# The order of VectorE and ScalarE in a gated-linear-attention mixer: weight subtractions and small steps change places

## The reference

```python
h = rmsnorm_2(x, mix_norm[l])
z = h @ w_in[l]
q_a, k_a, v_a, q_b, k_b, v_b, r_b, g_lr, gate_a, gate_b = split_cols(z, IN_SPLITS)
o_a = swa_attention(...)                    # sliding window, 8 heads
o_b = gla_attention(...)                    # gated linear attention, 4 heads
o_b = rmsnorm_2(o_b, gla_out_norm[l]...) * jax.nn.silu(r_b)
y_a = o_a @ w_proj_a[l]
y_b = o_b @ w_proj_b[l]
merged = jax.nn.sigmoid(gate_a) * y_a + jax.nn.sigmoid(gate_b) * y_b
x = x + merged @ w_out[l]
```

## Time and profile before

| | before |
|---|---|
| time of the runs, us | 2284.65, 2286.96, 2285.08 (median 2285.08) |
| the profiled execution | 2284.65 us, span of its records 2282.9 us |
| TensorE matmul | busy 2272.3 us of the span |
| TensorE weight load | busy 1931.9 us |
| VectorE | busy 1537.2 us |
| ScalarE | busy 1241.8 us |
| granted TensorE clock | 9 tenths or more in all 40 slices |
| DMA | mean 182 GB/s |

### The profile page before, as it was taken

The page is one execution under the profiler, slowest core; times in us unless marked ns, Lnnn a source line. Parts: engine busy times, 40 slices in busy tenths (PEclk is TensorE's granted clock), DMA queues, the critical chain, the costliest instruction groups (busy, mean ns, idle before and its releaser), DMA issues.

```text
span 2282.9 us, 29070 instructions
## 1 busy us (share of the span) xinstructions
PE 2272.3 (100%) x11756; PEld 1931.9 (85%) x11756; DVE 1537.2 (67%) x2156; ACT 1241.8 (54%) x1484; POOL 0.2 (0%) x4
## 2 busy tenths in 40 slices
PE   8999999999999999999999999999999999999999
PEld 7887888888888788888888888888888888888887
DVE  6764566765774466775776588767657747876773
ACT  6644445554653444654554576555555537754652
POOL 0000000000000000000000000000000000000000
PEclk9999999999999999999999999999999999999999
DMA  7556454564555455455555553645555555345553
GB/s 254 199 196 223 142 190 171 198 207 162 197 190 202 144 179 204 166 195 184 189 198 195 192 166 102 212 163 188 203 183 183 188 183 188 103 157 195 192 185 129
DMA packets 175802, 416.52 MB, mean 182 GB/s; under 512 B 16658, under 2 KB 21394, under 8 KB 175668
## 3 DMA queue, kind: packets, MB, share of 16 engines
q1 hardware_dynamic: 175380, 414.52, 53.0%
q10 hardware_dynamic: 288, 0.14, 0.0%
HBM read 413.55 MB, written 1.05 MB: 182 GB/s over the span
## 4 chain that ended last, share of the span: by engine, by line
PE 97%; DVE 1%; DMA 1%; ACT 1%; issue 0%; SPq 0%; DVEq 0%; ACTq 0%
PE psum L656 27%; PE psum L592 17%; PE psum L594 16%; PE psum L593 16%; PE psum L657 14%; PE psum L624 2%; PE psum L928 1%; PE psum L756 1%; DVE split_w L1581 0%; DMA raw<-t_gate_up_1a_dram 0%; PE psum L906 0%; DMA x<-x_dram 0%; PE psum L773 0%; ACT split_w L1129 0%; PE psum L897 0%
## 5 line engine op out<-in xcount | busy, mean ns | idle before, releaser
L1581 DVE TENSOR_TENSOR split_w<-raw,split_w 128x2048 fp32r<-128x2048 f32 (+2 forms) x408 | 886.4, 2178 | 308.8 <-ACT split_w L1129 307.8
L656 PE MATMUL psum<-xt,split_w 128*128 128x512 f32 x2816 | 982.0, 393 | 2.6 <-DVE split_w L1581 1.8
L1129 ACT ACTIVATE split_w<-raw 128x2048 fp32r<-128x2048 f32 (+2 forms) x408 | 741.0, 1824 | 325.2 <-PE psum L594 295.3
L657 PE MATMUL psum<-xt,split_w 128*128 128x256 f32 x2816 | 786.6, 279 | 0.0
L656 PEld LDWEIGHTS psum<-xt,split_w 128*128 128x128 f32 x2816 | 527.2, 187 | 123.4 <-DVE split_w L1581 2.2
L657 PEld LDWEIGHTS psum<-xt,split_w 128*128 128x128 f32 x2816 | 531.4, 189 | 0.3
L592 PE MATMUL psum<-split_w,xt 128*128 128x512 f32 (+1 forms) x736 | 291.1, 395 | 0.0
L594 PE MATMUL psum<-split_w,xt 128*128 128x512 f32 (+1 forms) x736 | 283.8, 386 | 0.0
L593 PE MATMUL psum<-split_w,xt 128*128 128x512 f32 (+1 forms) x736 | 283.6, 385 | 0.0
L592 PE MATMUL psum<-split_w,ht_hi 128*128 128x512 f32 x700 | 273.0, 390 | 0.0
L594 PE MATMUL psum<-split_w,ht_lo 128*128 128x512 f32 x700 | 272.5, 389 | 0.0
(11 more groups left out here) (272 smaller groups left out, 1731.1 us busy)
## 6 DMA issues: line engine op xcount, KB each, us to landing
raw<-w_in_dram SPq DMA_DIRECT2D x180, 512.0 KB, 4.4
raw<-t_gate_up_1b_dram SPq DMA_DIRECT2D x88, 512.0 KB, 4.1
raw<-t_gate_up_2a_dram SPq DMA_DIRECT2D x88, 512.0 KB, 4.1
raw<-t_gate_up_2b_dram SPq DMA_DIRECT2D x88, 512.0 KB, 4.1
raw<-t_gate_up_1a_dram SPq DMA_DIRECT2D x85, 512.0 KB, 4.2
raw<-ffn_w_down_dram SPq DMA_DIRECT2D x80, 512.0 KB, 4.3
raw<-w_a_dram SPq DMA_DIRECT2D x40, 512.0 KB, 4.1
raw<-w_b_dram SPq DMA_DIRECT2D x40, 512.0 KB, 4.2
```

Source lines behind the costliest of these rows:

```text
L656: nc.tensor.matmul(bank, whi[:, slot, w], xt[:, c, :, :], start=c == 0, stop=False)
L657: last = nc.tensor.matmul(bank[:, 0:T], wlo[:, slot, w], xt_hi[:, c, :], start=False, stop=c == DC - 1)
L1129: nc.scalar.activation(whi[:, u % HL, first:n], raw[:, r, first:n], ACT.Copy).then_inc(hi_done, 1)
L1581: nc.vector.tensor_tensor(wlo[:, u % HL, first:n], raw[:, r, first:n], whi[:, u % HL, first:n], ALU.subtract).then_inc(w_ready, 1)
```

## The change

Nothing is added or removed; eight calls change places, in the program of VectorE and of ScalarE. On VectorE, `turned(2)` goes ahead of `split(u0 + 23)`, `merge("a", 0, ...)` ahead of `split(u0 + 24)`, `merge("a", 1, ...)` ahead of `turned(3)` and both ahead of `split(u0 + 26)`, and `split(u0 + 27)` goes behind `gated(3)`, `out_norm()` and both `out_scaled()`; `split(u0 + 23)` goes behind `decayed(3, ...)` and `gated(1)` as well. On ScalarE, `sigmoids("b", 0, ...)` goes from behind `split(u0 + 28)` to behind `split(u0 + 27)`.

```diff
@@ mix2_scalar
                 split(u0 + 27)
+                sigmoids("b", 0, 1, u0 + 25)
                 out_squares(3)
                 so_root()
                 split(u0 + 28)
-                sigmoids("b", 0, 1, u0 + 25)
                 split(u0 + 29)
@@ mix2_vector
                 split(u0 + 22)
-                split(u0 + 23)
                 decayed(3, 0)
                 decayed(3, 1)
                 gated(1)
+                turned(2)
+                split(u0 + 23)
+                merge("a", 0, 2, u0 + 21)
                 split(u0 + 24)
-                turned(2)
-                merge("a", 0, 2, u0 + 21)
                 split(u0 + 25)
                 gated(2)
                 weights(3, 0)
                 weights(3, 1)
+                merge("a", 1, 0, u0 + 23)
+                turned(3)
                 split(u0 + 26)
-                turned(3)
-                merge("a", 1, 0, u0 + 23)
-                split(u0 + 27)
                 gated(3)
                 out_norm()
                 out_scaled(0, 2)
                 out_scaled(2, 4)
+                split(u0 + 27)
                 split(u0 + 28)
```

## The result

The changed kernel takes 2300.33 us (median of four executions, 2299.14 to 2301.11); the kernel before, run beside it, 2286.02 us (2284.65 to 2287.14). The ratio is 1.0057, 95% interval 1.0046 to 1.0069: slower by 13 us (10.5 to 15.8), where 10.8 were forecast, and the time lies 1.3 us above the range. The two medians are 14.3 us apart; the ratio agrees with the median of all 24 recorded executions of the changed kernel, 2298.95 us, rather than with that of the four. The profiled execution took 2298.62 us.

A forecast was written before the change was run, and what follows sets the result against it. TensorE's full stream of matmuls bounds the kernel. Waits of 2.40 and 3.00 us make 5.40 per layer, 10.8 over two layers; added to 2284.65 that is 2295.45, taken as 2295.5 us, range 2290.5 to 2299.

The forecast's parts named there:

- Place A: VectorE's `turned(2)` ahead of `split(23)`: TensorE loses 1.84 us at unit 23 and 0.56 at unit 24, 2.40 per layer.
- Place C: VectorE's `split(27)` behind `out_scaled`: TensorE loses 2.93 us at unit 27, about 0.07 more after it, 3.0 per layer.
- Place B: VectorE's `merge("a", 1)` and `turned(3)` ahead of `split(26)`: covered, costs nothing; without cover at most 1.5 us per layer.
- the sigmoids: ScalarE's sigmoids ahead of `out_squares(3)`: no delay, at most 0.1 us; value nothing.
- one place: Rival: only one of the two predicted TensorE stalls per layer appears, 2290.6 or 2289.5 us; chance 0.10.
- no difference: Rival: the stalls stay below what a measurement tells apart, or VectorE's order is not the code's, 2285 us; chance 0.05.
- a gain: Rival: TensorE's wait at the transposes of `merged` shortens by at most 1.0 us per layer, 2282.7 us; chance 0.01.
- the step on the clock: TensorE's granted clock stays at 1.00 after stalls of 1.8 and 2.9 us, so no time is added for slower matmuls.
- the rival with the clock: Rival: TensorE falls to 1.2 GHz after stalls at unit 27, costing 1.85 us each, 2299.2 us; chance 0.07.

The follow-up runs named there:

- the longer wait: Only `split(u0 + 27)` moved behind both `out_scaled()`, with VectorE's subtraction of unit 27 done twice, against the kernel before: 2299.81 us, ratio 1.0058.
- place C alone: Only `split(u0 + 27)` moved behind `gated(3)`, `out_norm()` and both `out_scaled()`, against the kernel before: 2294.50 us, ratio 1.0038.

## Why the prediction was wrong

**Right: what bounds the kernel, and the three places.** The stream of matmuls was full; no wait could be removed and three were made. Place A was given 1.84 and 0.56 us and measured 1.75 and 0.63. Place C was given 2.93 for the wait and 0.07 for the first matmul behind it, and measured 2.85 and 2.82, and 0.11. Place B and the sigmoids were given nothing and measured +0.2 us together. The sum was given 10.8 and measured 10.6 with the clock held up. The rivals of one place, of no difference and of a gain fall with the same runs.

**Wrong: the step on the clock.** The prediction took it that the granted clock stays at 1.00 behind the two stalls, so that the sum has no term for slower matmuls, because it had stayed after 1.24 us of waiting; it gave the fall 0.07. In its place the profiles show 0.50 behind the stall of place C in both layers, and 3.0 us lost to it. The row of 1.24 us couldn't carry the step: the wait of place C is more than twice as long. The runs put 1.78 us (clock held, both layers) and 2.82 us (it fell, both layers) beside it. The sixteen transposes at 0.23 us each after 3.97 us of waiting were the row nearest to a wait of 2.9, and should have been given about even chances. Their half pace shows in their time only: the window over them gives a granted clock of 1.00, but the trace holds no record of the clock ahead of 8.0 us. The same instruction, the transpose of the identity, took 0.11 us in the experiments above.

```profile
4.00:8.00 4.00, 3.64 (x16) 3.24 (x16) 1.52 (x4) 2.56 (x6) 0.00 (x0) 1.00 1.02 287
```

The price that the prediction took from them, 1.85 us per fall, was close: 1.5 measured in the changed kernel, and 2.3 and 1.4 behind the longer wait. The Trainium skill (TensorE: Matmul & The Clock Gate, "Part 1: The HAM clock gate") says that the array drops to half its clock when it idles and comes back under sustained work; the traces agree, with 0.43 against 0.23 us per matmul and a granted clock of 0.50.

**Also off: the base.** The sum stood on the profiled execution of 2284.65 us, which is the fastest of the four of before (three were known then, with a median of 2285.08); their median is 2286.02, 1.4 above. With it and the clock the steps give 2286.0 + 10.6 + 3.0 = 2299.6, against 2300.33. So the range missed by two terms at once: the rival with the clock ended at 2299.2 only because it stood on the fastest execution. And the miss of the range is narrow: it rests on the median of the four, and that of all 24 executions, 2298.95, lies just inside it.

**Still open.** The clock's share isn't the same in every execution. Of 24 executions of the changed kernel whose clock was recorded, nine show a mean of 0.998 and take 2300.8 us on average, seven show 0.999 and take 2299.0, and eight show 1.000 and take 2297.3, near the 2286.0 + 10.6 = 2296.6 of a clock that holds. A mean that rounds to 1.000 leaves at most 2.3 us at the lower level in both layers together, where the profiled execution had 3.4 in each. So the same waits didn't bring the clock down every time, and what decides it is open: only one execution of each kernel was profiled, and in the four kernels whose profile shows a fall it stands in both layers. Nor was it tried where between 1.78 and 2.82 us the clock begins to fall.

## What to carry to other kernels

Where one engine's stream is full, the order of a second engine's queue is worth nothing until something that the stream needs stands behind something that the stream itself releases; then it costs the time by which the answer comes later, less the margin that it had: with place C alone the subtraction of unit 27 ends 7.6 us later than before (where it ended at 1448.85), had 4.8 in hand, and cost TensorE 2.8. For each moved instruction, ask what it waits for now and whether the answer is the very engine that waits for it. And price a TensorE wait near three microseconds as the wait plus a likely stretch at the lower clock: here 2.8 us cost 4.4 with place C alone, and 1.8 us cost 1.9.

## What the runs showed of the hardware that had not been expected

- The lower clock can begin after the wait, with TensorE at work again: 0.8 us after it resumed in the changed kernel's first layer, 1.2 us after it in the second layer of place C alone. In the other six falls it began while TensorE was idle or as it resumed. In seven of the eight the lower level lasted 3.4 us; in the first layer of the longer wait it lasted 6.8.
- Twenty-eight transposes that nobody reads, issued into a free bank during an unavoidable wait, kept the clock at 1.00 and took 2.3 us off the tail (8.8 to 6.5). In the changed kernel twenty-six took off 3.0 (13.5 to 10.6).
- The profiled executions differed by up to 3.1 us before the mixer began, in a part in which all eleven kernels are the same, and the medians of the kernel before, timed beside the experiments, lay between 2285.64 and 2286.69 us. A difference of 1 us in the timed medians says little here; from a fixed instruction to the end the traces whose clock held agree with the waits counted in them within 0.3 us, save for the kernel with 28 transposes, which has 0.5 more.
